# Two of the four block sums of each weight chunk go from VectorE to accumulating DMAs

## What is computed

```
x = x + 1/2 * SwiGLU_a(RMSNorm(x))       # (silu(h @ w_gate) * (h @ w_up)) @ w_down, D_FF = 2816
x = x + Mixer(RMSNorm(x))                # layer 0: gMLP spatial gating, layer 1: latent attention
x = x + 1/2 * SwiGLU_b(RMSNorm(x))
```

## Time and profile before

| | |
|---|---|
| time, median of 3 (lowest, highest) | 2117.47 us (2117.15, 2117.64) |
| span of the profiled execution | 2115.8 us |
| TensorE busy in it | 2098.3 us, 99% |
| VectorE, ScalarE, GpSimd busy | 1523.0, 996.4, 145.2 us |
| DMA engines, hardware queue 1 / software queue 0 | 28.9% / 1.3% |
| granted TensorE clock, mean | 0.999 |

### The profile page before, as it was taken

How to read it: one execution, slowest core, us unless ns; L and a number is a source line. 1 busy time by engine, 2 the same in 40 slices (tenths; PEclk the granted TensorE clock), 3 DMA queues, 4 the chain that set the end, 5 groups by cost and what they waited for, 6 DMA issues and landing times.

```text
span 2115.8 us, 42925 instructions
## 1 busy us (share of the span) xinstructions
PE 2098.3 (99%) x17064; PEld 2036.3 (96%) x17064; DVE 1523.0 (72%) x2282; ACT 996.4 (47%) x1565; POOL 145.2 (7%) x155
## 2 busy tenths in 40 slices
PE   8999999999999999999999999999999999999999
PEld 8999999999999999999999999998768799999999
DVE  7887695336367879587978869579665568796783
ACT  6445353442135636255644535445563456354451
POOL 0000001222020000000000000111121210000000
PEclk9999999999999999999999999999999999999999
DMA  5233233322323333233332323341322133333232
GB/s 177 90 100 119 77 103 100 100 80 81 96 66 98 103 109 99 99 100 114 97 119 95 124 69 110 120 119 31 90 70 99 42 81 91 100 100 120 80 113 68
DMA packets 206228, 203.65 MB, mean 96 GB/s; under 512 B 12359, under 2 KB 201076, under 8 KB 205844
## 3 DMA queue, kind: packets, MB, share of 16 engines
q1 hardware_dynamic: 202938, 196.67, 28.9%
q0 software_dynamic: 2848, 4.86, 1.3%
q10 hardware_dynamic: 314, 0.37, 0.1%
HBM read 194.42 MB, written 2.66 MB: 93 GB/s over the span
## 4 chain that ended last, share of the span: by engine, by line
PE 97%; DVE 1%; ACT 1%; issue 0%; DMA 0%; SPq 0%; DVEq 0%
PE main L700 43%; PE side L749 23%; PE main L749 17%; PE side L1283 2%; PE main L1045 2%; PE main L1213 1%; PE side L1253 1%; PE side L1135 1%; PE main L1115 1%; PE side L959 1%; PE main L1292 1%; PE side L1085 1%; PE side L983 1%; PE main L1198 1%; PE main L1200 0%; PE main L1199 0%
## 5 line engine op out<-in xcount | busy, mean ns | idle before, releaser
L749 PE MATMUL side<-xw_hi,w_hi 128*128 128x260 f32 x1344 | 380.8, 283 | 0.9 <-DVE x L1936 0.8
L700 PE MATMUL main<-h_hi,w_lo 128*128 128x260 f32 x1888 | 380.1, 283 | 0.0
L700 PE MATMUL main<-h_hi,w_hi 128*128 128x260 f32 x1888 | 380.0, 282 | 0.0
L749 PE MATMUL side<-xw_hi,w_lo 128*128 128x260 f32 x1344 | 379.7, 283 | 0.0
L700 PE MATMUL main<-h_lo,w_hi 128*128 128x260 f32 x1888 | 379.3, 282 | 0.0
L749 PE MATMUL side<-xw_lo,w_hi 128*128 128x260 f32 x1344 | 378.2, 281 | 0.0
L700 PEld LDWEIGHTS main<-h_hi,w_hi 128*128 128x128 f32 x1888 | 290.8, 188 | 0.1
L700 PEld LDWEIGHTS main<-h_hi,w_lo 128*128 128x128 f32 x1888 | 290.7, 188 | 0.0
L700 PEld LDWEIGHTS main<-h_lo,w_hi 128*128 128x128 f32 x1888 | 290.1, 188 | 0.0
L749 PE MATMUL main<-xw_hi,w_hi 128*128 128x260 f32 x1008 | 286.8, 285 | 0.0
L749 PE MATMUL main<-xw_lo,w_hi 128*128 128x260 f32 x1008 | 285.8, 284 | 0.0
(11 more groups left out here) (450 smaller groups left out, 3619.7 us busy)
## 6 DMA issues: line engine op xcount, KB each, us to landing
raw<-in_ffn_w_up SPq DMA_DIRECT2D x44, 1024.0 KB, 5.2
raw<-in_ffn_w_gate SPq DMA_DIRECT2D x43, 1024.0 KB, 5.1
raw<-in_ffn_w_down SPq DMA_DIRECT2D x32, 1024.0 KB, 5.2
raw<-in_gmlp_w_in SPq DMA_DIRECT2D x16, 1024.0 KB, 5.4
raw<-in_ffn_w_down SPq DMA_DIRECT2D x16, 768.0 KB, 4.4
raw<-in_gmlp_w_out SPq DMA_DIRECT2D x8, 1024.0 KB, 5.2
raw<-in_mla_w_o SPq DMA_DIRECT2D x8, 1024.0 KB, 5.3
over<-in_cache_mla SPq DMA_DIRECT2D x64, 104.0 KB, 1.9
```

The costliest lines, as they stand in the source:

```text
L700: mm = nc.tensor.matmul(into[:, half, 0:HALF], w[:, k, m * P:(m + 1) * P], moving[:, k, half * HALF:(half + 1) * HALF], start=(k == 0 and ...
L749: mm = nc.tensor.matmul(into[j], w_tiles(w, j)[:, k, :], moving[:, k, j, :], start=(j in (0, 1) and k == 0 and i == 0), stop=(k == 3 and i ...
```

## The change

`sums_outer` is gone. SyncE loads the even row tiles' second block (W1) a second time, into `sums_w`, in pieces of 512 bytes. Then GpSimd issues two DMAs that add in place: W3 onto that copy (giving W3+W1), and W0 onto W1 in the `raw` slot itself (giving W0+W1). VectorE waits for the first (`inner_added`), ScalarE for the second (`outer_added`). The pair 4,5 is no longer contiguous, so its high part and its rest are two instructions of 512 elements each; for slot 1 the pair 1,2 lies in reversed order, which TensorE's index takes up.

```diff
+            def load_fast(slot, w, c0, free):
+                sp.wait_ge(lo_done, free)
...
+                sp.dma_start(raw[:, slot, :].rearrange("p (k c) -> p k c", k=KC), w_rows(w)[:, 0:KD, columns(c0, WC)])\
+                    .then_inc(raw_in[slot], 16)
+                sp.dma_start(added(2 * slot), w.rearrange("(i a p) n -> a p i n", p=P, a=2)[0][:, :, columns(c0 + P, P)])\
+                    .then_inc(outer_in[slot], 16)
...
+            def add_weights(s, raw_ready, w):
+                pool.wait_ge(raw_in[s], raw_ready)
+                pool.wait_ge(outer_in[s], 4 * (w - 2 * s) + 16)
+                pool.dma_start(added(2 * s), raw_block(s, 3), accum_op=ALU.add).then_inc(inner_added[s], 16)
+                pool.dma_start(raw_block(s, 1), raw_block(s, 0), accum_op=ALU.add).then_inc(outer_added[s], 16)
...
             def add_norm_squares(at):
                 for k in range(1, KD - 1):
+                    if k == 3:
+                        add_weights(0, 16 * (at.chunk // 2 + 1), at.wsum)
...
+            def sums_second(s, w, rested=None):
+                dve.wait_ge(inner_added[s], 4 * (w - 2 * s) + 16)
...
+                nc.vector.tensor_tensor(added(1), added(2 * s), raw_block(s, 0), ALU.add).then_inc(weights_summed, 1)
...
+            def fast_third(s, t, w):
+                act.wait_ge(tile_done, t)
+                act.wait_ge(outer_added[s], 4 * (w - 2 * s) + 16)
+                nc.scalar.activation(w_tiles(w_hi, 4), raw_block(s, 1), ACT.Copy)
                 act.wait_ge(weights_summed, w + 2)
+                nc.scalar.activation(w_block(w_hi, 5), sums_w[:, 3, :], ACT.Copy).then_inc(hi_done, 1)
...
+            def rest_third(s, l):
+                dve.wait_ge(hi_done, l)
+                take_rest(w_tiles(w_lo, 4), raw_block(s, 1), w_tiles(w_hi, 4))
+                take_rest(w_block(w_lo, 5), sums_w[:, 3, :], w_block(w_hi, 5), lo_done)
...
             def fast_chunk(...):            # VectorE
-                if after == "fast":
-                    sums_outer(1 - s, raw_ready, l + 4)
                 rest_raw(s, 6, 3, l + 5)
                 if after == "fast":
-                    sums_second(1 - s, w + 3)
+                    sums_second(1 - s, w + 2, l + 4)
```

More of the change, by code:

```diff
@@ L105, in ffn_past @@
                    evac=8 * fast + 4 * plain + 8 * groups, h=2 * pairs, act=2 * pairs, norm=1, rms=1, sums=0 if last else KD,
-                   snap=6 * fast, wsum=6 * fast, rows=2 * fast + 8 * groups, xg=16 + KD if plain else 17,
+                   snap=6 * fast, wsum=4 * fast, rows=2 * fast + 8 * groups, xg=16 + KD if plain else 17,
                    xh=20 + KD if plain else 21, blocks=16, added=0 if plain else 16 * (KD - 2),
@@ L481, in w_tiles, with raw_block, added, weights_at @@
             return w_block(w, j).rearrange("p (i c) -> p i c", c=P)
-        def raw_parts(s):
-            return raw[:, s, :].rearrange("p (i r c) -> p r i c", r=4, c=P)
+        def raw_block(s, r):
+            return raw[:, s, :].rearrange("p (i r c) -> p r i c", r=4, c=P)[:, r]
+        def added(b):
+            return sums_w[:, b, :].rearrange("p (i c) -> p i c", c=P)
+        def weights_at(s, j):
+            return 3 - j if s == 1 and j in (1, 2) else j
+        def added_pair(s):
+            return sums_w[:, s:s + 2, :].rearrange("p a c -> p (a c)")
         wkv_flat = wkv[:, :, :].rearrange("p h n -> p (h n)")
@@ L660, in _ @@
             spread_scales(1)
-            sp.wait_ge(os_done, 1)
+            sp.wait_ge(os_done, 2)
             load_out(0)
@@ L2157, in down @@
                 for i in range(4):
-                    if i == 2 and fast:
-                        sums_outer(n % 2, 16 * (n // 2 + 3))
                     if i == 3 and fast:
@@ L2734, in add_norm_squares, with ffn @@
                     pool.dma_start(square_sum[:], square[:, k % 2, :], accum_op=ALU.add).then_inc(sum_added, 16)
-            def ffn(after, final=False):
+            def ffn(at, after, final=False):
+                n, w = at.chunk, at.wsum
+                for g, pairs in enumerate(FF_GROUPS):
+                    rest = pairs - 2 if n == 0 else pairs
+                    for i in range(pairs - rest, pairs):
+                        if g or i:
+                            add_weights(0, 16 * (n // 2 + i + 1), w)
+                        add_weights(1, 16 * (n // 2 + i + 1), w + 2)
+                        w += 4
+                    n += 2 * pairs + 4
                 if final:
```

239 lines of the change are left out of this document (108 added, 131 removed).

## The result

The changed kernel takes 2207.75 us (median of 4 runs, 2205.43 to 2208.73); the kernel before took 2117.31 beside it (4 runs, 2115.89 to 2117.64). The ratio is 1.0426, 95% interval 1.0412 to 1.0441: slower by 90 us, where +24 was forecast. The direction was right and the time lies in the range given; the size was short by a factor of almost four.

The account below looks back on a forecast made before the run. TensorE was taken to bound the kernel. Stalls of 33.5 us from late adds, cut to 25, less 1 for the openings, gave +24 on 2117.5: 2141.5 us. The range was 2114 to 2235 us.

Parts of the forecast that it names:

- the line of a load and its adds: DMA path per chunk, from a load's first data to the end of its second add: 11.3 us.
- the beat: Gate and up stages: one chunk takes 10.1 us of TensorE's matmuls, so the next load's data start 10.1 us later.
- when it is needed: VectorE's wait for the first add: it may land 12.8 us after a gate load, 13.2 after an up load.
- Where the adds meet the next load: Shared DMA engines: each chunk's load is stretched by 1.2 us more; TensorE stalls 3.7 or 1.3 us a group, 33.5 together.
- The factor of three quarters: Taken on the 33.5 us of TensorE stalls because the overlap isn't complete, leaving 25 us.
- The openings: Three places where a SwiGLU block opens behind a norm: removing the outer sums gives back 1 us in all, bounds 0 and 3.
- Hidden: Rival for the DMA adds: an add costs only its bytes, 1.5 us, so nothing stalls; 2116.5 us, chance 0.37.
- The adds fill the engines: Rival for the 16 DMA engines: dearer adds fill them, 2234 or 2507 us; beyond 115 us, 0.18 shared with slow descriptor writing.
- milder case: DMA engines: 2.6 us an add and 1.28 for the second load, line 12.8 us, stalls 117 us, time 2234.
- harsher case: DMA engines: 6.1 us an add, 16.6 us needed per chunk of 10.1, 390 us lost, time 2507.
- Descriptor writing is slow: Rival on GpSimd: 3.4 us for 512 pieces, costing 130 us, 2247; beyond 115 us, 0.18 shared with adds filling the engines.
- more relief: Rival on VectorE's relief: missing matmuls of the openings and first group come back, 3 to 5 us; 2113 us, chance 0.05.

Follow-up runs that it names:

- the scratch kernels: Changed kernel, but VectorE makes both sums and the two DMA adds fill an unused tile: no wait 2122.97 us, first wait 2200.54, second 2192.64, both 2199.48.

## Why the prediction was right in direction and short in size

**What held.** That TensorE bounds the kernel and the relief of VectorE is worth nothing: 89 us less work, no gain. That the loss is a wait for adds which come late because the line of a load and its adds is longer than the beat, and that it starts afresh in each group: a chunk takes 11.5 us (forecast 11.3), the first add is in at 11.0 (10.9; 10.9 to 11.1 in the eight groups of four), and shortening the line takes the loss away. The DMA share of a window is 0.80, as forecast.

That the line came out so close is partly luck. Inside it an add is 2.40 for 2.0, the second load 1.23 for 1.0, GpSimd's start 0.5 for 0.1, and descriptor writing 1.28 for 1.8. With these sizes the same sum gives 3.15 + 1.23 + 0.65 + 0.5 + 1.28 + 0.6 + 2.4 + 2.4 = 12.2 us; 11.5 is measured, because the transfers overlap in part (the windows above).

**The step that failed first is "when it is needed".** It named the third evacuation, for which the second product of the next chunk waits, as the first thing TensorE asks for, and let the first add land as late as 12.8 or 13.2 us. But the seventh product of the running chunk already asks for the second evacuation (L2087, the first two rows of TensorE's waits), so the limits are 11.4 and 11.8. With the forecast's own line that alone makes 10.9 + 5 x 11.3 - (50.5 + 11.8) = 5.1 us in a group of four, and 10.9 + 33.9 - (30.3 + 11.8) = 2.7 in one of three: 49 us in place of 33.5. With 11.0 and 11.5 as measured, 6.2 and 3.4: 60 us. TensorE's waits behind L2087 and L1469 add up to 54.9.

**"Where the adds meet the next load" had only one direction.** It let each load be stretched by the adds ahead of it, and kept the add's own time from issue to landing as it is alone. The trace shows the other direction too: a first add that takes 4.3 us alone takes up to 8.8 when the next load is issued close behind it. Eight such chunks make 33.6 of the 64.5 us of stalls. So the agreement of 60 with 54.9 is no proof of the sum: it has the same growth in each group, while the stalls of the eleven groups are 3.2 to 10.6 us, openings included.

**Three more terms of the sum.** The factor of three quarters for an overlap that isn't complete had no row behind it; nothing was saved that way. The openings, put at -1, cost 9.6 us (three waits on L2049, the longest 4.8), two of them by such a meeting of the first add and the up load. The granted clock, for which the forecast has no term, costs 18, more than any other single term. Going from the +24 of the forecast to the measured 90: the due time brings 15 us, the measured line 11, the factor 8, the openings 11, the clock 18, together 63 of the 66 that were missing. By what TensorE's rows show, 54.9 + 9.6 + 18 = 82.5 of the 91 us between the two traces. A part of the rest is the restart: the product behind a stall takes 1.71 us in the chain above, where 1.44 is usual. That part was not measured by itself.

**The second wait.** The forecast put the second add 2 us behind the first and never asked when it is due. That it would be enough by itself to cost 70 us was not foreseen. In the scratch kernels it doesn't change the sum, since both waits end one chain. A repair of the first wait alone would have left it in place.

**The rivals.** *Hidden* (0.37) fell, and its condition was the right kind: with (scratch) adds of 2048-byte pieces the line is under the beat and the kernel is 11 us from the one before. The rule of the Trainium skill ("DMA: Bandwidth & Descriptors", "Why small descriptors are slow (HBM only)") says that transfers within SBUF don't pay for small pieces; that doesn't hold for these adds. The measurement decides: within SBUF, 256 KB cost (19.4% of 2197.1 - 27.5) / 168 = 2.37 us of the engines in pieces of 512 bytes and (15.1% of 2123.8 - 27.5) / 168 = 1.75 in pieces of 2048, and 72 us of the kernel's time go with the size of the pieces. No run here has a plain copy in small pieces. *The adds fill the engines* was closer than it looks: its milder case had 2.6 us for an add and 1.28 for the second load, the trace shows 2.40 and 1.23, and its price of 117 us is nearer to the measured 90 than the forecast's 24. Its harsher case (6.1 us an add, a DMA share near 1) fell. *Descriptor writing is slow* fell (1.28 us), and so did *more relief*.

## What to carry to other kernels

When a step moves from an engine to a queue, compare two things: the length of the whole line of transfers with the beat, and the landing of each with the moment at which the next engine is asked for whatever stands behind the wait. For the second, follow every instruction queued behind the wait, and take the first one that the bounding engine asks for, not the last. Then ask what the next load does to the transfer that is waited for, and not only what the transfer does to the load. A DMA may be waited for at no cost if it is issued as soon as its data are in and ends before the next load's data begin: the outer add cost 3 us so, and 59 when it was issued 4 us later, 0.9 us behind the next load.

## What was not expected of the hardware

- A transfer of GpSimd's queue isn't finished ahead of one that SyncE issues after it: both move together. An add under way when a 1 MB load begins lands after 10.2 us where it takes 5.4 at best, and the small load behind the big one after 7.64 where it takes 5.7 to 5.9 with one add a chunk. The nearer the load is issued behind an add, the later the add lands (4.3 us at a distance of 3, 8.3 at 0.8). So a late add makes the next one later still.
- GpSimd writes the descriptors of 512 pieces in 1.28 us, of 128 in 0.86, of 8 in 0.55: the slope from the two small sizes gave 1.8. The second of two such instructions shows 1.84 us, but starts 0.75 after the first.
- Single stalls of 2 to 6 us among busy stretches were followed by 3 to 7 us at the lower level of the granted clock (0.50 from 962 to 968 us, where it was 1.00 before): nine such stretches, a fifth of the loss.
